# Feed-forward up tiles: both of a pair in mixed passes of 512 and 256 columns, parts side by side

## What is computed

```python
S, D_MODEL, D_FF, FFN_CONV = 256, 1024, 2816, 3

def _causal_dwconv(x, w):          # position s sees s, s-1, s-2
    xp = jnp.pad(x, ((0, 0), (K - 1, 0), (0, 0)))
    y = xp[:, 0:S] * w[0]
    for j in range(1, K):
        y = y + xp[:, j:j + S] * w[j]
    return y

def _conv_glu_ffn(h, ffn_up, ffn_conv, ffn_conv_bias, ffn_down):
    u = _causal_dwconv(h @ ffn_up, ffn_conv) + ffn_conv_bias
    gate, val = jnp.split(u, 2, axis=-1)
    return (jax.nn.gelu(gate, approximate=True) * val) @ ffn_down
```

## Time and profile before

| what | value |
|---|---|
| median of 3 runs | 1070.45 us (1070.38 to 1070.77) |
| profiled execution | 1070.57 us, span 1068.6 us |
| busy in the span: TensorE, VectorE, ScalarE | 98%, 76%, 65% |
| granted TensorE clock, mean | 0.999 |
| feed-forward layers | about 182 to 362 us and 541 to 721 us of the span |

### The profile page before, as it was taken

One profiled execution on the slowest core, in us unless ns is written; L12 is line 12 of the kernel. 1 busy time (PEld: TensorE's weight loads), 2 busy tenths in 40 slices (PEclk: granted clock), 3 DMA queues, 4 the chain that ended last, 5 costly groups with the idle time before them and its releaser, 6 DMA issues.

```text
span 1068.6 us, 21008 instructions
## 1 busy us (share of the span) xinstructions
PE 1046.3 (98%) x7646; PEld 933.0 (87%) x7646; DVE 811.9 (76%) x1359; ACT 696.9 (65%) x1247; POOL 75.5 (7%) x113
## 2 busy tenths in 40 slices
PE   8999999999999999999999999999999999999997
PEld 8999788888889899988889988888989978888886
DVE  5856767888787896567688888786787769568995
ACT  6675666655555787568565555567975558457884
POOL 1002500000000000242030000000000000100000
PEclk9999999999999999999999999999999999999999
DMA  7643114656565455511456656564543326968991
GB/s 261 196 155 118 43 59 159 195 190 186 186 187 188 136 182 158 161 38 61 138 168 200 192 180 192 180 182 133 158 142 112 105 98 222 398 228 330 362 375 74
DMA packets 51688, 187.81 MB, mean 176 GB/s; under 512 B 6176, under 2 KB 6336, under 8 KB 51360
## 3 DMA queue, kind: packets, MB, share of 16 engines
q1 hardware_dynamic: 49104, 178.95, 50.9%
q0 software_dynamic: 2512, 7.88, 2.1%
HBM read 184.71 MB, written 3.67 MB: 176 GB/s over the span
## 4 chain that ended last, share of the span: by engine, by line
PE 84%; ACT 7%; DVE 6%; issue 2%; DMA 1%; POOLq 0%; POOL 0%; DVEq 0%; SPq 0%; ACTq 0%
PE bank L1860 20%; PE bank L1862 19%; PE bank L1861 19%; PE bank L1890 7%; PE bank L1970 4%; PE bank L1891 3%; ACT w L2356 1%; PE bank L1954 1%; DVE x L2728 1%; DMA ring<-wtiles 1%; PE bank L2163 1%; PE bank L2034 1%; DVE sq L2719 1%; DVE act L2711 1%; PE bank L964 1%
## 5 line engine op out<-in xcount | busy, mean ns | idle before, releaser
L2687 DVE TENSOR_TENSOR w<-ring,w 128x1024 fp32r<-128x1024 f32 x240 | 293.1, 1225 | 95.0 <-ACT w L2356 94.1
L2356 ACT ACTIVATE w<-ring 128x1024 fp32r<-128x1024 f32 x240 | 253.1, 1056 | 65.9 <-PE bank L1862 46.0
L1860 PE MATMUL bank<-act,w 128*128 128x256 f32 x800 | 229.4, 287 | 1.2 <-DVE w L2687 1.1
L1861 PE MATMUL bank<-act,w 128*128 128x256 f32 x800 | 226.4, 283 | 0.0
L1862 PE MATMUL bank<-act,w 128*128 128x256 f32 x800 | 226.4, 283 | 0.0
L1860 PEld LDWEIGHTS bank<-act,w 128*128 128x128 f32 x800 | 152.3, 190 | 6.3 <-issue 2.2
L1861 PEld LDWEIGHTS bank<-act,w 128*128 128x128 f32 x800 | 152.4, 191 | 0.3
L1862 PEld LDWEIGHTS bank<-act,w 128*128 128x128 f32 x800 | 152.4, 190 | 0.0
L1890 PE MATMUL bank<-act,w 128*128 128x512 f32 x336 | 120.2, 398 | 0.8 <-DVE w L2687 0.4
L1891 PE MATMUL bank<-act,w 128*128 128x256 f32 x336 | 94.2, 280 | 0.0
L1860 PE MATMUL bank<-w,hid 128*128 128x512 f32 x206 | 81.0, 393 | 0.0
(11 more groups left out here) (489 smaller groups left out, 2201.9 us busy)
## 6 DMA issues: line engine op xcount, KB each, us to landing
ring<-wtiles SPq DMA_DIRECT2D x240, 512.0 KB, 3.6
ring<-etiles SPq DMA_DIRECT2D x33, 512.0 KB, 5.7
act_raw<-etiles SPq DMA_DIRECT2D x33, 512.0 KB, 6.3
sq<-etiles SPq DMA_DIRECT2D x22, 512.0 KB, 5.8
cst<-etiles SPq DMA_DIRECT2D x8, 512.0 KB, 6.4
region<-packp POOLq DMA_DIRECT2D x4, 512.0 KB, 4.5
cst<-consts SPq DMA_DIRECT2D x1, 1176.5 KB, 11.2
x<-xt SPq DMA_DIRECT2D x2, 512.0 KB, 5.6
```

What stands on the lines that cost most here:

```text
L1860: t.matmul(out_, still[:, 0], moving[:, 0], start=first, stop=False)
L1861: t.matmul(out_, still[:, 0], moving[:, 1], start=False, stop=False)
L2356: a.activation(w_hi[:, s, :], ring[:, s, :], ACT.Copy).then_inc(hi_ready, 1)
L2687: v.tensor_tensor(w_lo[:, s, :], ring[:, s, :], w_hi[:, s, :].bitcast(F32), ALU.subtract).then_inc(lo_ready, 1)
```

## The change

`BESIDE` names both up tiles, so the second up tile of pairs 1 to 21 goes through `project_beside` too: 16 passes for 24, one more VectorE addition per pair (42 in the two layers), and ScalarE's and VectorE's order for that tile becomes that of the first. `act` now lies by block, hi and lo of a block side by side (2 KB), so that a 512-column pass reads one row; single parts are read as before, 256 columns in a row. `glu_s` moves from `region` to `mix`, which is not in use there; `x_parts` keeps its place and form under a name of its own.

```diff
-BESIDE = (0,)
+BESIDE = (0, 1)
...
-        act_both, act_hi, act_lo = split("act", KD, S)
+        act_pairs = ctx.enter_context(nc.sbuf_tensor("act", [P, KD, 2, S], F32R))
+        act_both = act_pairs[:].rearrange("p k b s -> p b k s")
+        act_hi, act_lo = act_both[:, 0], act_both[:, 1]
...
-        glu_s = region[:, 12 * S:12 * S + PAIRS * len(BESIDE) * S].rearrange("p (q w s) -> p q w s", q=PAIRS, s=S)
+        glu_s = mix[:, 0:PAIRS * len(BESIDE), :].rearrange("p (q w) s -> p q w s", q=PAIRS)
...
-        x_parts = act_both[:].rearrange("p b k s -> p b (k s)").rearrange("p b (c d) -> p b c d", c=NT)
+        x_parts = nc.alloc_sbuf_tensor_at("x_parts", [P, 2, NT, D], F32R, offset=places["act"])
...
                 for k in range(KD):
-                    still, moving = wblock(s, k), act_both[:, :, k, :]
-                    t.matmul(out_.rearrange("p (b s) -> p b s", b=2), still[:, 0], moving, start=k == 0, stop=False)
-                    mm = t.matmul(out_[:, 0:S], still[:, 1], moving[:, 0], start=False, stop=k == KD - 1)
+                    still, moving = wblock(s, k), act_pairs[:, k].rearrange("p b s -> p (b s)")
+                    t.matmul(out_[:, 0:2 * S], still[:, 0], moving, start=k == 0, stop=False)
+                    mm = t.matmul(out_[:, 0:S], still[:, 1], moving[:, 0:S], start=False, stop=k == KD - 1)
```

## The result

| kernel | median, us | runs | ratio to before, 95% interval |
|---|---|---|---|
| before | 1070.39 (1069.75 to 1071.6) | 9 | |
| after | 1073.67 (1071.98 to 1075.59) | 9 | 1.0029 [1.0021, 1.0038] |

The change costs 0.29%. That lies in the forecast's range (1068.3 to 1074.0), but not in the forecast's own band of 1071.4 to 1072.9: it is close to the time of the rival "slow rhythm" (1073.5). The prediction gave "slower by over 0.2%" 0.30 and "the same" 0.59.

A forecast was written before the change was run, and what follows sets the result against it. TensorE alone was taken to set the loop's pace, VectorE and ScalarE the layer edges. 1070.57 + 4.16 added - 2.52 saved = 1072.2, median 0.12 lower: 1072.1 us (own band 1071.4 to 1072.9, chance 0.50); range 1068.3 to 1074.0.

The forecast's parts named there:

- slow rhythm: Rival, loop's up tiles: mixed blocks in succession settle at 0.354 us, saving only 0.03 a pair; 1073.5 us; chance 0.17.
- The saving of 0.07 us a pair: TensorE, loop: second up tile takes 2.81 us like the first, not 2.88; 36 pairs save 2.52 us.
- point of decision, 0.056: Loop saving in us a pair from which downward the slower mixed-block rival decides: (4.16 - 2.14) / 36.
- The start: Each layer's start: VectorE's added addition delays the weight split that pair 3 awaits; 0.60 us a layer, 1.20 in all.
- The end: Each layer's end: last pair's addition and weight split delay the product and ScalarE's queue; 1.48 us a layer, 2.96 in all.
- Edges hidden: Rival, layer start and end: waits really belong to another engine, so only the saving is left; 1067.5 us; chance 0.10.
- The layout at nothing: Activation parts side by side, in up tiles and elsewhere: claimed to neither save nor cost time.
- Fast rhythm: Rival, loop: both up tiles run at 0.347 us a block, parts lying in one row; saves 5.0, 1069.6 us; chance 0.20.
- VectorE's cover of 0.35 us: Loop: VectorE's work plus forced idle step, about 8.0 us a pair, fits TensorE's 8.36 by some 0.35.
- VectorE becomes the bound: Rival, loop: VectorE needs 0.35 us more a pair than the rows give; 1075 us or more at 0.1 over; chance 0.03.
- The multiply-adds from SBUF at nothing: Second tile's two VectorE multiply-adds read SBUF instead of PSUM: 479 against 481 ns, counted as nothing.
- The sum that the prediction worked out from the Trainium skill: Loop tiles: N / 2.4 + 2.5 ns per pass, so one pass fewer saves 0.02 us a tile; 1073.9 us.

The follow-up runs named there:

- the repeat: The changed kernel run once more with no edit, beside the kernel before: 1073.24 us, ratio 1.0024.
- the doubled addition: Against the changed kernel: first and last pairs' second up tile as before, that tile's VectorE addition made twice in pairs 2 to 20; 1083.38 us.
- the two later comparisons: Against the kernel before: the changed kernel again, unedited, 1073.24 us; and the changed kernel with the old activation layout, 1073.12 us.

## Why the prediction came out as it did

- **The saving of 0.07 us a pair** is the term that was mis-sized, and the only one that matters. The step was "I take the first tile's present 2.81 for both". In the loop a mixed tile takes 2.81 behind a down tile, where its first block is short (227 + 113 ns); behind another mixed tile it takes eight full blocks of 353.7 ns on average, 2.83. Measured 0.046 a pair: 36 x 0.046 = 1.7 us where 2.5 stood. The rival named the mechanism ("mixed blocks one after another ... settle at pair 1's 0.354") and its evidence, and the prediction gave it 0.17. It over-priced it in its turn: it put the first tile at 2.83 as well, which the earlier trace rows already contradicted, since that tile's place did not change. Its point of decision, 0.056, holds: 0.046 lies below it, and the first comparison is slower by over 0.2%; the repeat, 0.24% with an interval from 0.15, leaves that open.
- **The start**: 0.60 predicted, 0.79 measured from addition to split. The order was read rightly; the product that now waits for its own multiply-adds was not costed. Pair 3 then runs 0.21 faster, not 0.07, so that net of that the start is near the 0.60. By pair 4 TensorE is the late one, as said.
- **The end**: 1.48 predicted, 1.42 measured; the product 1.50 later, where 1.49 was computed. "Edges hidden" falls: taking either edge back gave its price back.
- **The layout at nothing**: right, alone (1.0006) and with both tiles in passes (1073.12). "Fast rhythm" falls with it: pair 3 has it after its wait (second tile 2.77), and no later pair does.
- **VectorE's cover of 0.35 us**: right, by the doubled addition. "VectorE becomes the bound" falls.
- **The multiply-adds from SBUF at nothing**: right. In the steady loop those of 255 columns take 477 ns for the 479 and 481 of the earlier trace rows; the group's line has count, busy us and mean ns:

```profile
L3005 DVE SCALAR_TENSOR_TENSOR region<-mix,pf,region 128x255 f32<-128x255 f32 x29 | 13.8, 477 | 0.0
```

With the measured terms the prediction's sum is 2 x (0.81 - 0.21 - 0.80 + 1.42) = 2.4 us over before, where 1.6 stood. Added to the first median of before, that is 1072.8 us, still in the forecast's own band: the two later comparisons measured these 2.4 us (1073.24 for 1070.82, 1073.12 for 1070.73). The first one's 3.3 has an interval of 2.2 to 4.1, and its last 0.8 is not placed. That the measured 1073.67 lies so near the slow rhythm's 1073.5 is in part luck, since that rival counted a saving of 0.03 a pair where 0.046 was measured.

The sum that the prediction worked out from the Trainium skill (TensorE: Matmul & The Clock Gate, section "Back-to-back issue gap"), 1073.9, is nearer to the result than the forecast, but not for its reason. The section gives N / 2.4 + 2.5 as the gap of an isolated product, and says that it over-counts at 512 columns in a stream of weight loads and products; the prediction used it for such a stream. The trace does not agree with it: 512-column passes among their like start 227 ns apart, more than the 216 of the formula, the second tile's block went from 360 to 353.7 ns, 6.6 and not 2.5, and the same passes regrouped take 347 with no pass fewer.

## What to carry to other kernels

Price a tile by a row in which it stands behind the same neighbour that it will have, since the same sixteen passes took 2.81 us behind a down tile, 2.83 behind another mixed tile, and 2.77 in the pair behind a wait. When work is moved onto an engine that has room in the loop, look at the first and the last turn of the loop by themselves: here the cover was missing there, and a few instructions cost more than the whole loop saved. Such a change can be made for the inner turns alone, and that is what made it pay here.

## What the runs showed of the hardware

The order of passes of unequal length mattered in a loop without waits: 8 x (512, 256) in turn took 2.81 to 2.83 us, 8 x 512 and then 8 x 256 took 2.77 to 2.79; behind a wait of 1.06 us passes in turn took 2.77 too. The transition back cost something as well: the first five 512-column passes behind 256-column ones took 233, 236, 228, 233, 230 ns, then 227.

The granted clock fell in the middle of some executions. In the profiled execution of the changed kernel it was half of full, the 1.2 GHz level, for 3.4 us of the second block's gather. Windows there (busy us of each engine with instructions, granted clock, DMA), and what TensorE did before it fell:

```profile
893.00:898.00 5.00, 5.00 (x34) 4.46 (x32) 4.93 (x11) 3.36 (x4) 0.00 (x0) 1.00 0.59 171
898.50:901.70 3.20, 3.20 (x11) 3.10 (x10) 1.95 (x5) 1.43 (x3) 0.00 (x0) 0.50 0.91 311
```

```profile
895.08 0.95 PE L990 MATMUL bank<-region,pm 128*128 128x6 f32 x8
...
896.66 1.40 PE L990 MATMUL bank<-region,pm 128*128 128x6 f32 x12
...
898.90 7.07 PE L966 MATMUL bank<-pm,x_parts 128*128 128x384 f32 x32
```

Twenty products of only 6 columns stand just ahead of the fall; the gather's passes then start 320 ns apart and not 173, some 1.6 us lost in all. In the profiled execution of the kernel before, the same twenty products stand there and the clock stayed at 1.00, so they alone do not bring the fall. Five other profiled executions have a fall too, three of them (both tiles with the old layout, the end as before, the doubled addition) earlier in the second block, among products of 4 columns ahead of the gather. Beside the experiments, the mean clock was below 0.999 in 35 of 69 executions of the kernel before, in 8 of 12 with the layout alone, and in 15 of 22 of the changed kernel run again and the one with the old layout; in the first comparison it was in 8 of the changed kernel's 9. The executions at or above 0.999 show the difference as well (means of 1072.25 and 1072.70 us for 1070.58 and 1070.15). Whether the change makes the fall likelier, by shifting what stands there, is open.
